# Token-shift differences kept in another tile, and the key-norm sum one place later on TensorE

## What is computed

```python
def token_shift(z, mu):
    prev = jnp.pad(z[:, :-1], ((0, 0), (1, 0), (0, 0)))
    return z + (prev - z) * mu

z = h @ w_comb                                  # one projection for both halves
z_rwkv = token_shift(z[..., :N_SHIFT], shift_mu[i])
...
kk = heads(k * k_k)
kk = kk / jnp.maximum(jnp.sqrt(jnp.sum(kk * kk, axis=-1, keepdims=True)), 1e-12)
...
y = wkv7_scan(rh, heads(decay), kh, vh, -kk, kk * ah)
yn = ((y - mu) * lax.rsqrt(var + LNX_EPS)).reshape(bsz, s, c)
...
s_own = jnp.where(k_pos[None, :] <= q_pos[:, None], s_own, -jnp.inf)
p = jax.nn.softmax(...)
o = p @ v
```

## Time and profile before

| | |
|---|---|
| device time, median of 3 runs | 2645.99 us (2645.33 to 2646.06) |
| the profiled execution's own time | 2645.33 us |
| its span (first to last instruction) | 2643.7 us |
| TensorE busy | 2585.5 us, 98% of the span |
| VectorE busy | 1680.0 us, 64% |
| ScalarE busy | 1210.2 us, 46% |
| GpSimd busy | 116.4 us, 4% |
| mean granted TensorE clock | 0.994 |

### The profile page before, as it was taken

One profiled execution on the slowest core, in us unless ns is written; L12 is line 12 of the kernel. 1 busy time (PEld: TensorE's weight loads), 2 busy tenths in 40 slices (PEclk: granted clock), 3 DMA queues, 4 the chain that ended last, 5 costly groups with the idle time before them and its releaser, 6 DMA issues.

```text
span 2643.7 us, 48415 instructions
## 1 busy us (share of the span) xinstructions
PE 2585.5 (98%) x16267; PEld 2118.7 (80%) x16267; DVE 1680.0 (64%) x2761; ACT 1210.2 (46%) x1896; POOL 116.4 (4%) x183
## 2 busy tenths in 40 slices
PE   7999999999999999999899999999999999999998
PEld 6777777778888888888687777777788888888886
DVE  5767666657656556566567766676576565564665
ACT  5444445445434444344454444454454344443443
POOL 3000000000000000000010000100000000000000
PEclk9999999999999999999999999999999999999999
DMA  6443333365555555555544333333655655555554
GB/s 199 117 117 110 108 105 97 122 216 174 189 192 184 192 188 183 200 183 191 171 117 119 106 113 105 97 98 120 215 175 190 192 183 192 190 181 199 185 189 150
DMA packets 437898, 419.96 MB, mean 159 GB/s; under 512 B 19503, under 2 KB 351937, under 8 KB 437825
## 3 DMA queue, kind: packets, MB, share of 16 engines
q1 hardware_dynamic: 434176, 412.49, 49.1%
q0 software_dynamic: 3648, 6.52, 0.9%
HBM read 416.84 MB, written 2.10 MB: 158 GB/s over the span
## 4 chain that ended last, share of the span: by engine, by line
PE 91%; DVE 6%; ACT 1%; issue 1%; DMA 0%; DVEq 0%; SPq 0%; ACTq 0%
PE gemm_bank L514 29%; PE gemm_bank L515 15%; PE gemm_bank L539 11%; PE gemm_bank L541 11%; PE gemm_bank L540 11%; PE gemm_bank L517 2%; PE mix_banks L661 1%; PE mix_banks L687 1%; DVE b_rn L1267 1%; DVE b_wlo L1156 1%; PE mix_banks L694 1%; PE mix_banks L733 1%; PE mix_banks L737 1%; PE mix_banks L744 1%; PE mix_banks L740 1%
## 5 line engine op out<-in xcount | busy, mean ns | idle before, releaser
L1156 DVE TENSOR_TENSOR b_wlo<-b_raw,b_whi 128x1024 fp32r<-128x1024 f32 x777 | 940.2, 1223 | 561.0 <-ACT b_whi L892 558.8
L514 PE MATMUL gemm_bank<-b_hT,b_whi 128*128 128x512 f32 x3420 | 1253.5, 407 | 2.2 <-DVE b_zt L1162 2.2
L892 ACT ACTIVATE b_whi<-b_raw 128x1024 fp32r<-128x1024 f32 x777 | 810.1, 1057 | 609.2 <-PE gemm_bank L541 428.4
L515 PE MATMUL gemm_bank<-b_hT,b_wlo 128*128 128x256 f32 x3648 | 1012.7, 281 | 0.0
L514 PEld LDWEIGHTS gemm_bank<-b_hT,b_whi 128*128 128x128 f32 x3420 | 643.2, 188 | 171.3 <-issue 22.4
L515 PEld LDWEIGHTS gemm_bank<-b_hT,b_wlo 128*128 128x128 f32 x3648 | 689.5, 189 | 10.7
L539 PE MATMUL gemm_bank<-b_whi,b_mT 128*128 128x512 f32 x1280 | 501.6, 392 | 0.0
L541 PE MATMUL gemm_bank<-b_whi,b_mT 128*128 128x512 f32 x1280 | 498.3, 389 | 0.0
L540 PE MATMUL gemm_bank<-b_wlo,b_mT 128*128 128x512 f32 x1280 | 498.2, 389 | 0.0
L539 PEld LDWEIGHTS gemm_bank<-b_whi,b_mT 128*128 128x128 f32 x1280 | 240.3, 188 | 51.3 <-issue 1.4
L541 PEld LDWEIGHTS gemm_bank<-b_whi,b_mT 128*128 128x128 f32 x1280 | 240.3, 188 | 50.3
(11 more groups left out here) (238 smaller groups left out, 1895.8 us busy)
## 6 DMA issues: line engine op xcount, KB each, us to landing
b_raw<-in_w_up SPq DMA_DIRECT2D x256, 512.0 KB
b_raw<-in_w_down SPq DMA_DIRECT2D x256, 512.0 KB
b_raw<-in_w_in SPq DMA_DIRECT2D x384, 256.0 KB
b_raw<-in_w_out SPq DMA_DIRECT2D x60, 512.0 KB
b_raw<-in_w_in SPq DMA_DIRECT2D x8, 512.0 KB
b_xt<-in_x SPq DMA_DIRECT2D x4, 512.0 KB, 6.0
b_raw<-in_w_out SPq DMA_DIRECT2D x8, 256.0 KB
out<-b_xt SPq DMA_DIRECT2D x8, 256.0 KB, 2.3
```

The source lines that it names most:

```text
L514: mm(bank[b0 + b][:, :], whi[r][:, cols], pair, start=first, stop=False)
L515: m = mm(bank[b0 + b][:, 0:SEQ], wlo[r][:, cols], act[:, kt, 0, :], start=False, stop=False)
L892: f(whi[r][:, :], raw[r][:, :, :].rearrange("p a b -> p (a b)"), ACT.Copy).then_inc(hi_done, 1)
L1156: tt(wlo[r][:, :], flat(raw[r][:, :, :]), whi[r][:, :].bitcast(F32), ALU.subtract).then_inc(lo_done, 1)
```

## The change

The three differences no longer go to `kf`, `ta` and `xs[:, 1]` but to columns 0 to 767 of `yof`, where G of the pair before lies. So the first two may not be written before TensorE has read that G. For this GpSimd waits for a new semaphore `x_free` (it takes the place of `col_zero` in the start-up), which TensorE raises with the first of the two V transposes of each pair. `pt` moves to columns 768 to 1151. On TensorE `key_norms(n + 1)` moves from behind the V transposes to behind the attention output product.

```diff
-        pt = yof[:, 0:384]
+        pt = yof[:, 768:1152]
...
-        dsh = (ta[:, :], kf[:, :], xs[:, 1, :])
+        dsh = yof[:, 0:3 * SEQ].rearrange("p (a b) -> p a b", b=SEQ)
...
-            nc.gpsimd.memset(ldc[:, :, 0:1], 0.0).then_inc(e["col_zero"], 1)
+            nc.gpsimd.memset(ldc[:, :, 0:1], 0.0).then_inc(e["x_free"], 1)
...
             def unit(l, i, n, tiles, after):
                 pool.wait_ge(tile_out, tiles - 2)
+                pool.wait_ge(e["x_free"], n + 1)
                 for j in (1, 0):
-                    nc.gpsimd.tensor_tensor(dsh[j], zt[:, j, 0:SEQ], zt[:, j, 1:SEQ + 1],
+                    nc.gpsimd.tensor_tensor(dsh[:, j, :], zt[:, j, 0:SEQ], zt[:, j, 1:SEQ + 1],
                                             ALU.subtract).then_inc(e["diffed"], 1)
                 pool.wait_ge(e["pair_done"], n + 1)
                 pool.wait_ge(tile_out, tiles)
-                nc.gpsimd.tensor_tensor(dsh[2], zt[:, 2, 0:SEQ], zt[:, 2, 1:SEQ + 1],
+                nc.gpsimd.tensor_tensor(dsh[:, 2, :], zt[:, 2, 0:SEQ], zt[:, 2, 1:SEQ + 1],
                                         ALU.subtract).then_inc(e["diffed"], 1)
...
                 for u in range(2):
                     m = turned(mb[1][:, P * u:P * u + P], zt[:, 5, 1 + P * u:1 + P * u + P], ident)
-                m.then_inc(e["va_turned"], 1)
-                if more:
-                    key_norms(n + 1)
+                    m.then_inc(e["va_turned"] if u else e["x_free"], 1)
                 pe.wait_ge(e["probs"], V)
...
                 mm(mb[1][:, P:2 * P], vt[:, 1, :], pt[:, 2 * P:3 * P], start=False, stop=True).then_inc(e["o_sum"], 1)
+                if more:
+                    key_norms(n + 1)
                 fill(2)
...
-                    stt(sh[:, j, :], dsh[j], col(MU + PAIRS * j), zt[:, j, 1:], ALU.mult,
+                    stt(sh[:, j, :], dsh[:, j, :], col(MU + PAIRS * j), zt[:, j, 1:], ALU.mult,
                         ALU.add).then_inc(e["shifted"], 1)
...
-                stt(sh[:, 2, :], dsh[2], col(MU + PAIRS * 2), zt[:, 2, 1:], ALU.mult,
+                stt(sh[:, 2, :], dsh[:, 2, :], col(MU + PAIRS * 2), zt[:, 2, 1:], ALU.mult,
                     ALU.add).then_inc(e["shifted"], 1)
```

More of the change, by code:

```diff
@@ L227, in trunk @@
                  "u_sum", "u_out", "s_sum", "s_tmp", "s_out", "y_sum", "y_mean", "y_cen", "y_sq", "y_var", "y_root",
-                 "y_rinv", "y_norm", "y_turned", "y_gain", "y_bonus", "y_scaled", "y_gated", "y_hi", "col_zero",
+                 "y_rinv", "y_norm", "y_turned", "y_gain", "y_bonus", "y_scaled", "y_gated", "y_hi", "x_free",
                  "swapped", "roped_c", "roped_s", "roped", "va_turned", "va_out", "score_sum", "masked", "smax",
@@ L1472, in parameters @@
                 dve.wait_ge(clears, 2)
-                dve.wait_ge(e["col_zero"], 1)
+                dve.wait_ge(e["x_free"], 1)
             for l in range(DEPTH):
```

## The result

The changed kernel takes 2717.49 us (median of 4 runs, 2716.47 to 2718.49) against 2645.66 us for the kernel before in the same session: a ratio of 1.0271, with a 95% interval of 1.0253 to 1.0289. It is 71.8 us slower. The forecast was 2716.5 us.

A forecast was written before the change was run, and what follows sets the result against it. TensorE bounds the kernel, with each passage's path from L968 over ACT and DVE having no slack. 58.7 us of later roots plus 12 of clock make 70.7 on 2645.33, 2716.0, given as 2716.5; range 2696 to 2728 for 8 in 10.

The forecast's parts named there:

- The release and its wake-up: Between pairs, the first V transpose releases GpSimd at 108.54; GpSimd starts at 108.63, with 0.09 us for every wake step.
- The hold: DVE's first operation on the differences is held until GpSimd's second subtraction ends, 0.47 us more a passage.
- TensorE's lateness: TensorE loads the probabilities at 111.84 in place of 108.70, 3.14 us late, and stands idle for 3.2 us.
- The root of the key norms: ACT's root L968 starts at 115.12 in place of 110.93, making the next pair 4.19 us late: 58.7 us over 14.
- The clock: Stalls put TensorE at half clock for 3.4 us in 9 of 14 passages, 1.3 us each: 12 us.
- Rival A: TensorE's clock stays up behind the new stalls: 2704.7 us, chance 0.20.
- rival C: The clock falls in every passage for the whole 6.9 us, 1.8 us a passage: 2730 us, chance 0.10.
- Rival B: Slack between L968 and L639 absorbs the extra key-norm delay; only TensorE's 3.47 us counts: 2694.6 us, chance 0.10.
- Rival D: Not slower: TensorE takes the probabilities 0.33 us earlier without key norms in front: 2641.4 us; D or no change 0.05.
- The signs: Expected profile: pairs 4.2 us longer, up to 5.5 where the clock falls; 3.5 us or less means wrong.

The follow-up runs named there:

- useless work in the stall: The changed kernel with 20 extra transposes of a constant block, whose results nothing reads, in front of TensorE's wait for probs: 2697.07 us, ratio 1.0195.

## Why the prediction came out as it did, step by step

The forecast of 2716.5 us is 1 us off, but this is partly luck: two terms were off by 8 us each, in opposite directions. The mechanism, DVE held by a late release with the softmax queued behind it, was right.

- **The release and its wake-up** were right: GpSimd starts 0.37 us behind the start of the first V transpose (0.28 + 0.09), as forecast. GpSimd to DVE takes 0.16 us, not the 0.09 taken for every step.
- **The hold** was right in kind and too large: 0.22 us where 0.47 was put in. The longer wake-up takes back a part of that: the reciprocal is 3.21 us late in the first passage and 3.12 to 3.20 in the others (3.33 forecast).
- **TensorE's lateness** was over-sized. I shifted the weight load of the transposes (108.70), but its matmuls used to wait behind the key-norm sum, and this wait is gone from there. With the clock up (useless work in the stall) they start 3.41 us behind the V transposes, against 0.66 before: 2.75 late, not 3.14.
- **The root of the key norms**, and so the chain, is 3.7 us late with the clock up (6.4 against 2.67 for most passages), where 4.19 was forecast. The sum of this term is 14 x 4.19 = 58.7 in the forecast and 51.1 in the run (2697.07 less 2645.93). The wait alone makes the root 2.87 us late and the sum alone 0.62, 3.5 together; the last 0.2 come only with both.
- **Which part is which**: the moved sum alone is 7.8 us; the other 43 us vanish, and the clock's price with them, when DVE no longer queues the softmax behind the differences. So the cause of the loss is the order on DVE: a wait for a late release, placed in front of work that was on time.
- **The clock** was right in kind and under-sized: 12 us forecast, 20.4 measured. It fell in 12 passages where I took 9. The price of 1.3 us was nearly right for a fall of 3.4 us (1.3 to 1.6 by the pair lengths), but three falls last 6.8 us and cost 2.6 each, so the mean is 1.7. Rival A, that it stays up, fell; rival C, that it always falls for the whole length, came true in no passage but three.
- **Rival B** (slack behind the root) fell: the sum moved alone, with no stall of TensorE, costs 7.8 us, and with the clock up the changed kernel is 51.1 us slower, more than TensorE's own lateness of 3.1 us a passage (44) gives. The waits at L639 and L649 have not grown by 0.7 us, though, as I wrote: part of the slack shows as a longer wait of the first tick behind the small matmuls for DVE's sums (5.0 us in total, 2.2 before).
- **Rival D** fell; the release comes too late in every passage, and DVE's reciprocal is 3.1 to 3.2 us later for it.
- **The signs.** The pairs are 4.9 to 6.3 us longer where the clock falls and 3.6 where it doesn't, where 4.2 was forecast and up to 5.5 with a fall. With 3.5 us as the sign of a wrong chain, the 3.6 came close to it.

## What to carry to other kernels

When a buffer is shared with a tile that is read last by a late instruction, look at what is queued behind the first user of the release, not at the work itself: here two subtractions of 0.6 us cost 43 us with the clock up, because the softmax stood behind them on DVE, and nothing once it didn't. A stall of TensorE can have a second price, the clock that falls behind it, and this price can be told from the waiting by filling the stall with useless transposes. Useful work in the stall is not the same test: it may only move the wait to its own inputs. And a forecast that comes out right should still be taken apart: its terms may have cancelled.

## What the runs showed of the hardware

- In this kernel idle times of TensorE of about 3 us between dense matmuls were followed by 3.4 or 6.8 us at 1.2 GHz in most cases, not in all: 12 of 14 with 3.0 us of idling, 8 of 14 with 2.4 us and a sum behind it, 14 of 14 with 3.3 us. With two ticks taken into the stall, which left 1.6 us of idling, it was none of 14, and so with 20 small transposes, which left 0.84 us.
- A fall of the clock that follows such a stall costs this kernel 1.7 us of its time on average: 1.3 to 1.6 us when it lasts 3.4 us, 2.6 us when it lasts 6.8 us.
- 0.36 us more of stall in each passage cost 10 to 11 us in all, of which 5 are the stall itself; the rest came with two more falls of the clock and five more long ones.
- A DVE operation with two operands in SBUF that starts during a GpSimd subtraction took 0.70 us in place of 0.48. The Trainium skill, page "SBUF — State Buffer", section "SBUF: two separate sides", has it blocked until the GpSimd instruction is through; the subtraction ended 0.42 us after the shift began (109.85 + 1.18 = 111.03 for the pair of them, against 110.61), and the shift grew by 0.22 us only. The measurement decides: the hold was about half of what was left of the subtraction.
